# A mixture-of-experts encoder: the router moved between projection products, job 0's rows found on their own

## The reference

```
x = x + merged @ w_out
h = rmsnorm(x) * norm_ffn                      # per row
logits = h @ w_router + b_router               # 1024 -> 32 experts
top_v, top_i = top_k(logits, 4);  gate = softmax(top_v)
for each chosen expert e of a row:
    gu  = h @ w_gate_up[e] + b_gate_up[e]      # 1024 -> 2048
    g   = min(gu[:1024], 7);  lin = clip(gu[1024:], -7, 7)
    y  += gate * ((g * sigmoid(1.702 g) * (lin + 1)) @ w_down[e] + b_down[e])
out = rmsnorm(x + y) * norm_final
```

## Time and profile before

| | us |
|---|---|
| median of 3 runs | 1692.56 (1691.78 to 1693.84) |
| profiled execution, its own time | 1692.21 |
| its span in the trace | 1690.4 |
| PE busy | 1602.7 |
| DVE busy | 1290.0 |
| ACT busy | 1100.7 |
| POOL busy | 335.4 |

### The profile page before, as it was taken

How to read it: one execution, slowest core, us unless ns; L and a number is a source line. 1 busy time by engine, 2 the same in 40 slices (tenths; PEclk the granted TensorE clock), 3 DMA queues, 4 the chain that set the end, 5 groups by cost and what they waited for, 6 DMA issues and landing times.

```text
span 1690.4 us, 21687 instructions
## 1 busy us (share of the span) xinstructions
PE 1602.7 (95%) x7613; PEld 1176.3 (70%) x7613; DVE 1290.0 (76%) x1017; ACT 1100.7 (65%) x1037; POOL 335.4 (20%) x260
## 2 busy tenths in 40 slices
PE   5999899999948999999999999999999999999993
PEld 4877788888735777677777677777777777777772
DVE  6746644334558989998989989889989899988881
ACT  5446753233326778777778777777777787777762
POOL 6300000000011222233222232222232222332210
PEclk7999999999968999999999999999999999999997
DMA  8320002315737999999999999999999999999963
GB/s 254 125 75 19 1 1 89 110 65 183 289 118 267 348 371 377 382 368 365 371 381 376 375 367 364 375 371 385 370 368 372 372 374 381 367 365 373 377 253 118
DMA packets 101653, 475.98 MB, mean 282 GB/s; under 512 B 10912, under 2 KB 11440, under 8 KB 68720
## 3 DMA queue, kind: packets, MB, share of 16 engines
q1 hardware_dynamic: 93408, 448.17, 69.1%
q0 software_dynamic: 7888, 27.23, 7.0%
q10 hardware_dynamic: 320, 0.08, 0.0%
HBM read 456.67 MB, written 19.66 MB: 282 GB/s over the span
## 4 chain that ended last, share of the span: by engine, by line
PE 92%; DVE 4%; DMA 2%; ACT 2%; issue 1%; POOL 0%; SPq 0%; ACTq 0%; POOLq 0%; DVEq 0%
PE ps L1622 27%; PE ps L1643 14%; PE ps L1625 14%; PE ps L1648 7%; PE ps L1370 6%; PE ps L1372 6%; PE ps L1371 6%; PE ps L1395 4%; PE ps L1489 2%; DVE l_w L1150 2%; PE ps L1614 2%; PE ps L1463 2%; PE ps L1634 1%; PE ps L1454 1%; DMA x_sb<-in_x 1%; DMA xg<-h_rows,gather_row 1%
## 5 line engine op out<-in xcount | busy, mean ns | idle before, releaser
L1150 DVE TENSOR_TENSOR l_w<-a_w,h_w 128x2048 fp32r<-128x2048 f32 x384 | 866.4, 2284 | 37.2 <-ACT h_w L782 36.3
L782 ACT ACTIVATE h_w<-a_w 128x2048 fp32r<-128x2048 f32 x384 | 732.7, 1916 | 246.1 <-PE ps L1625 182.8
L1622 PE MATMUL ps<-h_w,xt_hi 128*96 128x512 f32 x1024 | 287.4, 402 | 0.4 <-DVE xt_lo L1296 0.4
L1622 PE MATMUL ps<-h_w,xt_lo 128*96 128x512 f32 x1024 | 278.7, 394 | 0.0
L1625 PE MATMUL ps<-l_w,xt_hi 128*96 128x512 f32 x1024 | 278.5, 393 | 0.0
L935 POOL TENSOR_TENSOR mark_sb<-ones 1x1 f32<-1x1 f32 x96 | 99.2, 1033 | 862.2 <-ACT y_sb L834 832.4
L1622 PEld LDWEIGHTS ps<-h_w,xt_lo 128*96 128x96 f32 x1024 | 165.9, 162 | 71.6
L1625 PEld LDWEIGHTS ps<-l_w,xt_hi 128*96 128x96 f32 x1024 | 165.7, 162 | 71.4
L1622 PEld LDWEIGHTS ps<-h_w,xt_hi 128*96 128x96 f32 x1024 | 163.9, 163 | 69.7 <-issue 1.1
L1643 PE MATMUL ps<-h_w,at_hi 128*96 128x512 f32 x512 | 168.3, 410 | 0.0
L1643 PE MATMUL ps<-h_w,at_lo 128*96 128x512 f32 x512 | 160.2, 394 | 0.0
(11 more groups left out here) (217 smaller groups left out, 1674.9 us busy)
## 6 DMA issues: line engine op xcount, KB each, us to landing
a_w<-in_w_gate_up SPq DMA_DIRECT2D x256, 1024.0 KB, 7.6
a_w<-in_w_down SPq DMA_DIRECT2D x128, 1024.0 KB, 6.3
w_raw<-in_w_in SPq DMA_DIRECT2D x8, 2048.0 KB, 8.9
w_raw<-in_w_out SPq DMA_DIRECT2D x2, 2048.0 KB, 9.2
x_sb<-in_x SPq DMA_DIRECT2D x4, 512.0 KB, 6.1
w_raw<-in_w_in SPq DMA_DIRECT2D x2, 1024.0 KB, 17.1
w_raw<-in_w_mem_kv SPq DMA_DIRECT2D x1, 2048.0 KB, 13.8
x<-in_x SPq DMA_DIRECT2D x4, 512.0 KB, 5.0
```

The costliest lines, as they stand in the source:

```text
L782: nc.scalar.activation(h_w[m % H_SLOTS][:], a_w[m % A_SLOTS][:], ACT.Copy).then_inc(wh_done, 1)
L1150: nc.vector.tensor_tensor(l_w[m % A_SLOTS][:], a_w[m % A_SLOTS][:], h_w[m % H_SLOTS][:].bitcast(F32), ALU.subtract).then_inc(wl_done, 1)
L1622: nc.tensor.matmul(ps[0:SLOTS, n, :], x_part[:, k, :], w_h[:, n * COLS:(n + 1) * COLS], start=False, stop=False)
```

## The change

- The logits come from the residual. `router_g` = `router_w` * `norm_ffn` (the gain as a third row of `gains`); `turn_x2` turns `x2` itself; `route` multiplies with `x2_t` held in the array and `router_g` moving, so logits come out with rows on partitions; `take_top` multiplies them by the row's rstd and adds the bias. `turn_logits` and `add_router_bias` are gone.
- Turn and route of block t-1 stand inside row block t of gemm 17, ahead of k = 2 and k = 5. Only block 3's come after it. DVE's `moe_low(0, 1)` is moved into the first block.
- Job 0's rows are found from the ranks alone: expert 0's block 0 is job 0, its slot is the rank of the row among those that chose expert 0. `rank_0`, `slot_hot_0` and four small products give `gather_row` directly; `gather(0)` is issued after that. POOL fills `expert_gu` for job 0 itself.
- The other tables come later: blocks, places and `job_table` on DVE between that and `low_xt(0)`; `number_hots` (DVE) after `moe_low(0, 2)`; `job_vals` as two operations on POOL; the sixteen products in PE's `gate_up` of job 0 after k = 4; `take_slots` (DVE) after `moe_low(0, 6)`. ACT's parts 6 and 7 wait for `vals_ready`, gather 1 for `slots_ready`. The tables lie at new addresses.
- `stay_awake(n)`: n products of 128 x 128 of ones into an unused bank, behind each small step of PE.
- SP begins the stream after `xg_in[0]` (gather 0 landed) in place of `slots_ready`.

```diff
-            sp.dma_start(router_b[:], b_router[0].rearrange("(e a) -> e a", a=1)).then_inc(router_in, 16)
+            sp.dma_start(router_b[:], b_router.to_broadcast([P, N_EXP])).then_inc(router_in, 16)
...
             sp.wait_ge(table_ready, 1)
-            sp.wait_ge(slots_ready, 1)
+            sp.wait_ge(xg_in[0], 16)
...
+            act.dma_start(gain_rows[2 * KD:3 * KD, :], norm_ffn[0].rearrange("(k p) -> k p", p=P)).then_inc(gains_in, 16)
...
             for t in range(TB):
                 square(t)
-                if t == TB - 1:
-                    act.wait_ge(gemm_ps, G1)
-                    moe_high(0, 2)
-                if t:
-                    take_h2(t - 1)
-            moe_high(0, 3)
-            take_h2(TB - 1)
+                take_x2(t)
+                root(t)
+            act.wait_ge(gemm_ps, G1)
+            moe_high(0, 2)
...
-            for m in (4, 5):
+            for m in (3, 4, 5):
                 moe_high(0, m)
-            act.wait_ge(table_ready, 1)
-            act.wait_ge(slots_ready, 1)
-            act.wait_ge(hot_b_ready, 1)
             act.wait_ge(limits_ready, 1)
             nc.scalar.activation(mark_act[:], ones[0:1, 0:1], ACT.Copy).then_inc(y_ready, 1)
-            name_gu(0)
+            take_xt(0)
+            act.wait_ge(table_ready, 1)
+            act.wait_ge(vals_ready, 1)
             for m in (6, 7):
                 moe_high(0, m)
-            take_xt(0)
...
+            pool.wait_ge(row_0_ready, 1)
+            gather(0, gather_row[:, 0:1])
+            nc.gpsimd.memset(mark_pool[:], 0.0).then_inc(expert_gu_ready, 1)
...
+            pool.wait_ge(hots_ready, 2)
+            step.link(nc.gpsimd.tensor_tensor(job_vals[:, :, 0, :], job_hots[:], spread(dest_vals[:, :, 0], NJ), ALU.mult))
+            nc.gpsimd.tensor_tensor(job_vals[:, :, 1, :], job_hots[:], spread(dest_vals[:, :, 1], NJ), ALU.mult).then_inc(vals_ready, 1)
             pool.wait_ge(slots_ready, 1)
-            for j in range(2):
-                keep_row(gather_row[:, j:j + 1], j)
-                pool.wait_ge(rows_kept, j + 1)
-                gather(j)
+            gather(1, slot_rows[:, 1:2])
...
             for t in range(TB):
                 add_x(1, t)
+                if t == 0:
+                    moe_low(0, 1)
+                take_x2(t)
                 norm_h2(t)
...
                 take_top(t)
+                choose(t)
             dve.wait_ge(place_ps, 1)
+            step.link(nc.vector.scalar_tensor_tensor(out=rank_0[:].rearrange("p (t a) -> p t a", a=1),
+                                                     in0=ps[:, 0, 0:P].rearrange("p (t e) -> p t e", t=TB)[:, :, 0:1], scalar=1.0,
+                                                     in1=chosen[:, :, 0:1], op0=ALU.add, op1=ALU.mult))
...
+            dve.wait_ge(row_0_ps, 1)
+            step.link(nc.vector.tensor_scalar(row_miss_0[:], ps[0:SLOTS, 2, 0:1], 0.0, cols[0:SLOTS, 4:5], ALU.is_equal, ALU.mult))
+            nc.vector.scalar_tensor_tensor(out=gather_row[:, 0:1], in0=row_miss_0[:], scalar=-1.0, in1=ps[0:SLOTS, 2, 0:1],
+                                           op0=ALU.add, op1=ALU.add).then_inc(row_0_ready, 1)
...
-            for m in (1, 2):
-                moe_low(0, m)
             low_xt(0)
+            moe_low(0, 2)
+            number_hots()
             for m in range(3, LOW_LEAD):
                 moe_low(0, m)
+            take_slots()
...
+                    last = nc.tensor.matmul(ps[:, 4 + t, 0:N_EXP], x2_t[:, k, :], router_g[:, k, :], start=k == 0, stop=k == KD - 1)
+                last.then_inc(lg_ps, 1)
+
+            def router_between(t, k):
+
+                if t and k == 2:
+                    turn_x2(t - 1)
+                if t and k == 5:
+                    route(t - 1)
...
+            gemm(17, h_hi, h_lo, lambda t: None, between=router_between)
+            turn_x2(TB - 1)
+            route(TB - 1)
+            stay_awake(6)
...
+            stay_awake(3)
+            pe.wait_ge(hot_0_ready, 1)
+            for t in range(TB):
+                last = nc.tensor.matmul(ps[0:SLOTS, 2, 0:TOP_K], slot_hot_0[:, t, :], dest_vals[:, t * TOP_K:(t + 1) * TOP_K, 0],
+                                        start=t == 0, stop=t == TB - 1)
+            last.then_inc(row_0_ps, 1)
+            stay_awake(4)
...
+            def slot_tables(k):
+                if k == 4:
+                    pe.wait_ge(vals_ready, 1)
...
-            pe.wait_ge(slots_ready, 1)
-            pe.wait_ge(table_ready, 1)
             pe.wait_ge(xg_in[0], 16)
             turn_tokens(0)
-            gate_up(0, 0, 0, lambda k: None)
+            pe.wait_ge(table_ready, 1)
+            gate_up(0, 0, 0, slot_tables)
```

More of the change, by code:

```diff
@@ L233, in encoder_kernel @@
         dest_vals = small("dest_vals", [P, CHOICES, 2], F32)
-        row_miss = small("row_miss", [SLOTS, NJ], F32)
+        rank_0 = small("rank_0", [P, TB], F32)
+        slot_hot_0 = small("slot_hot_0", [P, TB, SLOTS], F32)
         assert at <= 128 * KIB
[L238 to L241, removed]
+        slot_hot = sb("slot_hot", [P, CHOICES, SLOTS], F32, 174 * KIB)
+        job_vals = sb("job_vals", [P, CHOICES, 2, NJ], F32, 180 * KIB)
+        job_hots = sb("job_hots", [P, CHOICES, NJ], F32, 187 * KIB)
         A_AT = (96, 104, 64, 72, 80, 88, 32, 40, 48, 56, 144, 152)
@@ L1286, in _ @@
[L1286 to L1291 removed]
+            dve.wait_ge(dve_chain, step.n)
@@ L1372, in three, with gemm @@
                 return nc.tensor.matmul(bank, lo, w_hi, start=False, stop=stop)
-            def gemm(u, hi, lo, free, ks=None, ready=None):
+            def gemm(u, hi, lo, free, ks=None, ready=None, between=None):
                 n_k = UNIT_K[u]
@@ new lines, in route, with stay_awake @@
+                last.then_inc(lg_ps, 1)
[4 more added lines that the diff above has]
+                    route(t - 1)
+            def stay_awake(n):
+                for _ in range(n):
+                    nc.tensor.matmul(ps[:, 5, 0:P], ones[:], ones[:], start=True, stop=True)
+            gemm(17, h_hi, h_lo, lambda t: None, between=router_between)
+            turn_x2(TB - 1)
+            route(TB - 1)
@@ L1589, in _ @@
             turn(1, P, blocks_start[:].rearrange("p g e -> p (g e)")).then_inc(blocks_ps, 1)
-            for c in range(CHOICES):
-                pe.wait_ge(vals_ready, c // TOP_K + 1)
-                last = nc.tensor.matmul(ps[0:SLOTS, 3, 0:2 * NJ], slot_hot[:, c, :], job_vals[:, c, :, :].rearrange("p v j -> p (v j)"),
-                                        start=c == 0, stop=c == CHOICES - 1)
-            last.then_inc(slots_ps, 1)
-            pe.wait_ge(hot_ready, 1)
-            nc.tensor.matmul(ps[0:1, 2, 0:NJ], cols[0:N_EXP, 6:7], job_hot[0:N_EXP, :], start=True, stop=True).then_inc(hot_ps, 1)
+            stay_awake(3)
+            pe.wait_ge(hot_ready, 1)
+            nc.tensor.matmul(ps[0:1, 3, 0:NJ], cols[0:N_EXP, 6:7], job_hot[0:N_EXP, :], start=True, stop=True).then_inc(hot_ps, 1)
+            stay_awake(4)
+            def slot_tables(k):
+                if k == 4:
+                    pe.wait_ge(vals_ready, 1)
+                    for c in range(CHOICES):
+                        last = nc.tensor.matmul(ps[0:SLOTS, 5, 0:2 * NJ], slot_hot[:, c, :], job_vals[:, c, :, :].rearrange("p v j -> p (v j)"),
+                                                start=c == 0, stop=c == CHOICES - 1)
+                    last.then_inc(slots_ps, 1)
             def turn_tokens(s):
```

201 lines of the change are left out of this document (93 added, 108 removed).

## The result

| | before | after |
|---|---|---|
| median (lowest to highest), us | 1692.51 (1691.78 to 1693.84, 4 runs) | 1681.13 (1679.76 to 1682.05, 4 runs) |
| profiled execution, us (span) | 1692.2 (1690.4) | 1681.96 (1680.1) |
| PE's granted clock, mean of the profiled span | 0.975 | 0.981 |

The ratio is 0.9934, 95% interval 0.9922 to 0.9947: 11.4 us faster, where 15.5 (1676.7) was forecast. The time lies in the range.

The account below looks back on a forecast made before the run. PE, 95% busy, was taken as the bound, with gains only in the wait chain before job 1: -6.7 - 14.6 - 5.2 + 11.0 = -15.5 us, from 1692.2 to 1676.7; range 1670.5 to 1684.

Parts of the forecast that it names:

- A: Router between gemm 17's products: choice done at about 467.2 in place of 473.9, 6.7 us gained.
- rival 3: The router's DVE chain overruns its slot by a microsecond and three turns wait: 3 us more, 1679.7; chance 8%.
- B: Job 0's rows found on their own: choice to gather issue 2.9 us in place of 17.5.
- the six `stay_awake` products end at about 466.1, one us before: Between choice and gather: idle PE products end one us ahead of the place products, priced at 0.9.
- C: First gather's issue to job 0's tokens ready: 9.0 us in place of 14.2, no weight loads beside it.
- plus 1.8 for the first issue: First gather: 1.8 us added to a landing of 4.1 for POOL's first issue, giving 5.9.
- D: Job 0, end of `xt_lo` to job 1's start: about 42.0 us in place of 31.0, 11.0 lost.
- The second gather, issued at 499, has until 516 to land and be turned; even 11.9 fits: Job 0, behind `take_slots`: second gather hidden before job 1 at about 521.1, even with a landing of 11.9.
- Rival 1: Job 0: POOL does not block DVE and starts at once; only 2.4 us come back, 1674.3; chance 17%.
- rival 2: The first gather lands in 10.7 whatever runs beside it: 4.8 us more, 1681.5; chance 12%.
- rival 4: Job 0: POOL's two `job_vals` products become the bound, 19 us instead of 3.6 to decide; 1694 at 21; chance 4%.
- the head of D: First part of job 0, from end of `xt_lo` (479.1) to end of `take_slots` (498.9).

Follow-up runs that it names:

- x10: Changed kernel with the second gather issued only once `moe_low` 9 has ended; 1680.81 us in one execution.
- x11: Changed kernel in which DVE copies parts 7 to 9 of job 0 instead of subtracting (output not the reference's); 1675.71 us in one execution.
- x5: Changed kernel without its 20 idle `stay_awake` products; 1681.02 us, 0.9938 of the kernel before.
- x4: Changed kernel with the two products of `job_vals` on DVE in place of POOL; 1679.13 us, 0.9932 of the kernel before.
- x9: Changed kernel with `job_vals` on DVE, slot tables after part 3, and DVE held until POOL has read the second gather's offsets; 1676.74 us, 0.9910 of before.
- x1: Changed kernel, but DVE waits after `take_slots` until POOL has issued the second gather; 1679.21 us, 0.9924 of the kernel before.
- x8: Changed kernel with a one-element DVE copy behind each of `moe_low` 7, 8 and 9; 1680.80 us, 0.9937 of the kernel before.
- x7: Kernel before, with its next weight loads started only when the first gather has landed; 1687.56 us, 0.9974 of the kernel before.

## Why the prediction came out as it did

Job 1 was forecast at 521.1 and came at 525.87; the 4.8 us between are nearly the whole miss (4.4 on the median, 5.3 by the profiled execution). From job 1 to the end it took 1154.2, as before (1153.8).

**A, choice done: 467.2 forecast, 470.39 measured.** The mechanism held: three turns and three routes fit between the products without a stall, and rival 3 is out. The term that was mis-sized is the route, taken as 1.3 between the ends of 0.5 and 1.9. PE in gemm 17, where the next product starts 1.70 behind the route's first (answers to the earlier trace rows):

```profile
443.42 1.87 PE L1571 MATMUL ps<-router_g,x_t 128*128 128x32 f32 x16
445.12 0.47 PE L1380 MATMUL ps<-w_high,h_hi 128*128 128x512 f32 x1
```

The moving columns had fallen to a quarter, and the time hardly at all: 16 instructions at 0.107 us, which is the pace of the turns (8 in 0.87), each of them with 128 stationary columns. I had the row for it and took a value below it. Three routes make 1.2. Another 1.35 came in from upstream: gemm 0 began 0.2 later, and the mean granted clock from 23 to 36 us was 0.64 in place of 0.74. No edit there explains it, and it isn't the change's: the last `add_x` of gemm 16 ends at 434.54 in after and at 433.19 in before, but at 432.93 to 435.77 in the other kernels that have the same program up to there. In x10 and x11, where it ends at 433.07 and 432.93, the choice is done at 468.88 and 468.77, 1.6 to 1.7 behind the forecast. The rest, 0.6, is three turns of 0.87 in place of 0.8 and 0.3 behind the last product.

**B, choice to gather: 2.9 forecast, 4.46 measured.** The order of the steps is as predicted. One step that failed is "the six `stay_awake` products end at about 466.1, one us before": they did not hold the clock. The granted clock was 0.64 from 469 to 470 and 0.50 from 470 to 472 with them running, so the place products took 0.90 + 0.43, and the three idle products ahead of the rows stand on the path with 1.16 (chain, 471.78), 0.4 of it behind the end of `slot_hot_0`. x5 shows what they are good for: they bring the clock back by 474. What the clock cost is read from x4, which had it full: B was 3.82 there (469.87 to 473.69), so the clock is 0.6 of the miss of 1.56. The other 0.9 are sizes: POOL's 0.82 from `row_0_ready` to the issue, where I gave 0.2 to handovers, and the eight row products, 0.86 in x4 where I took 0.6.

**C, gather to tokens: 9.0 forecast, 6.85 measured.** Landing 4.08, and nothing added to it. The term "plus 1.8 for the first issue" is wrong: no first-use price shows. In the kernel before, the 2.34 and 2.73 of the earlier trace rows were POOL waiting for the end of a `moe_low`; here, beside DVE operations of 0.13 to 0.49 us, the first gather takes 0.98. The same misreading stood in D. The next weight loads began at 481.95, 9.95 sooner than before (491.90) and not 16.

**D, job 0: 42.0 forecast, 44.2 measured.** Two errors of opposite sign. The first made it shorter: POOL started `job_vals` at once, at 486.63, not 2.2 later, and `take_slots` ended 17.8 behind `xt_lo` where 19.8 was forecast. POOL's two products did hold DVE: `moe_low` 4 and 5 took 3.76 each, 1.5 more than 2.28, while POOL's 3.65 and 3.60 are the rest of a `moe_low` and 1.5 of work. That is the whole-instruction lock of the Trainium skill (SBUF — State Buffer, section "SBUF: two separate sides"), by which DVE pays all of POOL's work, two times 1.5; x4 measures 3.0, and the trace agrees.

The step that failed and made it longer is "The second gather, issued at 499, has until 516 to land and be turned; even 11.9 fits". The bound was taken from landings, counted from an issue that takes its usual time, and the issue itself took 19.3. It cost 4.04 us of DVE. I had written down that POOL and DVE collide and applied it to POOL's large products only, the work whose own time is long; but an instruction of 0.9 us needs its turn as well, and which turn it gets was the question. The same section of the Trainium skill warns that a DVE operation in a two-port mode can keep POOL from writing the descriptors of a transfer. It also counts a DVE operation with two SBUF inputs among those that block a POOL instruction which reads SBUF, for one instruction at a time. The subtractions here are of that second kind, but no single instruction explains 19.3 us: eight boundaries went by, that of the clamp among them, before POOL got in at the ninth. The measurement goes beyond the rule.

Rival 1 was half right (POOL started at once, but did block), rival 2 wrong for the first gather, rival 4 looked at the right engine but at the wrong instruction. None gave the time by its mechanism.

**Luck.** The sum came nearer than its terms. C (9.0 for 6.85) and the head of D (19.8 for 17.8) were 4.1 too long, most of it by first-use starts that don't exist; the second gather's issue left 4.04 out. That the two cancel is luck: with the first alone put right, the forecast would have been about 1672.6, and the miss 8.5.

**What stays open.** What the short stop at the head of the row changes. A row that begins without one isn't always shut: `moe_low` 3 to 6 follow `slot_hot` without a stop, and both `job_vals` got in at a boundary. With `take_slots` directly ahead, whose small operations read PSUM, it was shut in every kernel of the change without the stop, up to the operation behind the last `moe_low` (518.2 in after). What makes that place different was not tried.

## What to carry to other kernels

A POOL instruction, and an indirect DMA's issue is one, needs a turn between DVE's: where DVE has a long row without waits, look at POOL's own time in the timeline, not only at the landing, and where it is as long as the row, let DVE wait at its head for its own last operation (0.04 us here, with the slot tables moved as well, took 16.4 us off the gather and the 4.0 us of waiting off the path). An instruction that seems dear at its first use is first to be compared with what ended at the same moment on another engine. Small matmuls are priced by how many there are: 0.107 us each for 128 stationary by 32 moving columns and for the turns' 128 by 128, 0.12 for the old route's 32 by 128.

## What the runs showed of the hardware that was not expected

- A gather's issue took 0.93 and 0.95 us with DVE standing (x9, x1), 0.98 beside its small operations, 2.7 to 2.9 with one `moe_low` to wait for, and 19.3 beside an unbroken row behind `take_slots`. One-element copies in the row (x8) don't open it, copies in place of subtractions (x11) don't either.
- Idle products of 128 columns didn't keep the granted clock from falling to 0.50 (470 to 472 in after), but it was back at 1.00 from 474 with them and not by 488 without (x5). In x4 it did not fall there at all.
- Four weight loads of 1 MB issued ahead of a gather of 96 rows put 4.8 us on its landing (10.71 against 5.93, x7).
- A copy of 128x2048 fp32 on DVE took 1.22 us, the subtraction with two inputs 2.28 (x11).
